# Second-block attention in head pairs: row halves for scores, scaled probabilities, values as the stationary operand on column halves

## The reference

```python
def global_gqa(q, k, v, k_ctx, v_ctx):            # layer 0, kind "G"
    ...
        sc = jnp.einsum('bqkgd,bnkd->bkgqn', q_blk, k_all).astype(jnp.float32) * scale
        p = jax.nn.softmax(sc, axis=-1).astype(v_all.dtype)
        return jnp.einsum('bkgqn,bnkd->bqkgd', p, v_all)

def windowed_gqa(q, k, v, k_ctx, v_ctx, sink_logit):   # layer 1, kind "W"
    ...
        p = jax.nn.softmax(jnp.concatenate([s_loc, s_ctx, s_sink], axis=-1), axis=-1)
    ...
# neighbourhood_attention, layer 1, kind "N": the same with a position bias and no sink
y = jnp.concatenate([y_a * jax.nn.silu(ag), y_b * jax.nn.silu(hg)], axis=-1)
x = x + gate[:, None] * jnp.matmul(y, w_out[layer])
```

## Time and profile before

| | us |
|---|---|
| median of 3 runs (1758.97 to 1762.38) | 1761.64 |
| span of the profiled execution | 1749.0 |
| TensorE (PE) busy | 1610.5 (92%) |
| VectorE (DVE) busy | 970.5 (55%) |
| ScalarE (ACT) busy | 785.3 (45%) |
| share of the chain that ended last: PE, DVE, ACT | 74%, 14%, 6% |
| mean granted TensorE clock | 0.956 |

### The profile page before, as it was taken

One profiled execution on the slowest core, in us unless ns is written; L12 is line 12 of the kernel. 1 busy time (PEld: TensorE's weight loads), 2 busy tenths in 40 slices (PEclk: granted clock), 3 DMA queues, 4 the chain that ended last, 5 costly groups with the idle time before them and its releaser, 6 DMA issues.

```text
span 1749.0 us, 20908 instructions
## 1 busy us (share of the span) xinstructions
PE 1610.5 (92%) x8012; PEld 1243.0 (71%) x8012; DVE 970.5 (55%) x1725; ACT 785.3 (45%) x1329; POOL 46.8 (3%) x105
## 2 busy tenths in 40 slices
PE   3899998799989999987999989999968999889997
PEld 3787777699878877776998717677733572676666
DVE  2554457566455544566664426744777731784664
ACT  2444785455344447854553314344420011533552
POOL 4000000000000000000000000000000000310000
PEclk8899999899999999988999999999979999898999
DMA  8653333476545532326665473311210025742000
GB/s 193 241 184 105 108 110 120 121 193 199 191 165 181 178 121 97 121 97 168 169 193 193 169 264 97 98 49 49 73 48 1 0 73 194 221 121 72 25 25 25
DMA packets 188838, 220.94 MB, mean 126 GB/s; under 512 B 20505, under 2 KB 117445, under 8 KB 188672
## 3 DMA queue, kind: packets, MB, share of 16 engines
q1 hardware_dynamic: 186532, 211.98, 38.2%
q0 software_dynamic: 2208, 7.63, 1.8%
HBM read 216.57 MB, written 3.01 MB: 126 GB/s over the span
## 4 chain that ended last, share of the span: by engine, by line
PE 74%; DVE 14%; ACT 6%; issue 3%; SPq 2%; DMA 0%; ACTq 0%; DVEq 0%
PE bank L570 19%; PE bank L572 18%; PE bank L571 18%; PE bank L835 5%; PE bank L896 2%; DVE w_low L1487 2%; SPq L2142 2%; ACT w_high L1125 2%; PE bank L922 2%; PE bank L907 2%; PE bank L730 1%; PE bank L676 1%; DVE arena L1800 1%; PE bank L707 1%; PE bank L1001 1%
## 5 line engine op out<-in xcount | busy, mean ns | idle before, releaser
L1487 DVE TENSOR_TENSOR w_low<-raw,w_high 128x1024 fp32r<-128x1024 f32 x352 | 424.9, 1217 | 422.0 <-ACT w_high L1125 421.0
L1125 ACT ACTIVATE w_high<-raw 128x1024 fp32r<-128x1024 f32 x352 | 366.6, 1046 | 338.0 <-PE bank L572 338.0
L570 PE MATMUL bank<-w_high,acts_r 128*128 128x512 f32 (+1 forms) x896 | 361.6, 404 | 45.6 <-DVE w_low L1487 22.6
L572 PE MATMUL bank<-w_high,acts_r 128*128 128x512 f32 (+1 forms) x896 | 351.4, 392 | 0.0
L571 PE MATMUL bank<-w_low,acts_r 128*128 128x512 f32 (+1 forms) x896 | 350.6, 391 | 0.0
L570 PEld LDWEIGHTS bank<-w_high,acts_r 128*128 128x128 f32 x896 | 173.4, 194 | 85.6 <-DVE w_low L1487 26.9
L570 PE MATMUL bank<-acts_r,w_high 128*128 128x256 f32 (+1 forms) x736 | 230.0, 313 | 0.0
L571 PE MATMUL bank<-acts_r,w_high 128*128 128x256 f32 (+1 forms) x736 | 223.6, 304 | 0.0
L572 PE MATMUL bank<-acts_r,w_low 128*128 128x256 f32 (+1 forms) x736 | 223.6, 304 | 0.0
L572 PEld LDWEIGHTS bank<-w_high,acts_r 128*128 128x128 f32 x896 | 172.6, 193 | 37.4
L571 PEld LDWEIGHTS bank<-w_low,acts_r 128*128 128x128 f32 x896 | 173.1, 193 | 32.6
(11 more groups left out here) (261 smaller groups left out, 1806.0 us busy)
## 6 DMA issues: line engine op xcount, KB each, us to landing
raw<-in_w_in SPq DMA_DIRECT2D x70, 1024.0 KB, 5.1
raw<-in_w_up SPq DMA_DIRECT2D x64, 512.0 KB, 5.5
raw<-in_w_down SPq DMA_DIRECT2D x32, 1024.0 KB, 4.8
raw<-in_w_ada SPq DMA_DIRECT2D x24, 1024.0 KB, 5.2
raw<-in_w_in SPq DMA_DIRECT2D x32, 512.0 KB, 4.9
raw<-in_w_o SPq DMA_DIRECT2D x8, 1024.0 KB, 5.0
raw<-in_w_out SPq DMA_DIRECT2D x8, 1024.0 KB, 4.9
raw<-in_w_out_c SPq DMA_DIRECT2D x4, 768.0 KB, 5.1
```

The lines of the kernel that those rows point to most:

```text
L570: mm(o, lh, rh, start=start, stop=False)
L572: return mm(o, ll, rh, start=False, stop=stop)
L1125: run(A_(high, src, ACT.Copy), (high_ready, n + 1))
L1487: run(V.tensor_tensor(low, src, high.bitcast(F32), ALU.subtract), (split_ready, n + 1))
```

## The change

Units come in pairs: two heads, one even and one odd, on the same tile. The step of the loop on each engine is now a pair. TensorE does both scores one behind the other (even head on rows 0 to 63 of its array, odd head on 64 to 127), then both turnings, then twice the features, then the values of pair p-2. There the values are stationary (128 x 64) and the turned probabilities move, 128 columns; the even head's output goes to partitions 0 to 63 and the odd head's to 64 to 127 of one bank, block by block in turn. The output has features on its partitions. VectorE multiplies the probabilities by the inverse of the sum in place (`scale_probs`) before they are turned, and TensorE waits for that (`probs_scaled`). ScalarE copies one output per pair. `turn_outputs` is gone, and VectorE multiplies by the gate from SBUF. `S` and `PT` have two buffers as before. Lines of the changed program have other numbers: L897 is the scores, L908 the turning, L927 the values, L1123 ScalarE's copy, L1350 the exponential of layer 0, L1116 the rounding, L1821 and L1823 the scaling.

```diff
@@ -150,8 +150,8 @@
 def units_of_block2(layer):
 
     if layer == 0:
-        return [("G", h, t) for h in range(QH) for t in range(T4)]
-    return [(k, h, t) for k in ("W", "N") for h in range(QH) for t in range(TILES)]
+        return [("G", 2 * hp + e, t) for hp in range(QH // 2) for t in range(T4) for e in range(2)]
+    return [(k, 2 * hp + e, t) for k in ("W", "N") for hp in range(QH // 2) for t in range(TILES) for e in range(2)]
 
 
 def half_list():
@@ -426,7 +426,8 @@
-        sum_inverted = Signal(sem("sum_inverted"), softs)
+        sum_inverted = Signal(sem("sum_inverted"), [k for k in b1u if kinds[k] != "C"])
+        probs_scaled = Signal(sem("probs_scaled"), b2u)
...
@@ -901,52 +902,44 @@
                     return range(2, 4) if kind == "G" and t >= TILES else range(4)
 
                 def second(u):
-                    pe.wait_ge(*probs_at(2 + l, u))
+                    pe.wait_ge(*probs_scaled.at(2 + l, u))
                     o = open_bank("p", 2 + l, u, 0, among=ATTENTION_BANKS)
                     for n, _ in enumerate(blocks_of(u)):
                         ins = tr(o[:, n * P:(n + 1) * P], S[:, u % 2, n * P:(n + 1) * P], ident[:, :])
                     close_bank(ins, "p", 2 + l, u, 0)
 
-                def values(u):
-                    kind, h, t = U[u]
-                    pe.wait_ge(*emptied("p", 2 + l, u, 0))
-                    o = open_bank("o", 2 + l, u, among=ATTENTION_BANKS)
-                    blocks = blocks_of(u)
+                def values(p):
+
+                    for u in (2 * p, 2 * p + 1):
+                        pe.wait_ge(*emptied("p", 2 + l, u, 0))
+                    o = open_bank("o", 2 + l, p, among=ATTENTION_BANKS)
+                    blocks = blocks_of(2 * p)
                     for n, b in enumerate(blocks):
-                        if kind == "G":
-                            v = kv2[:, b, (KVH + h // 4) * DH:(KVH + h // 4 + 1) * DH]
-                        elif kind == "W":
...
+                        for u in (2 * p, 2 * p + 1):
+                            kind, h, t = U[u]
+                            if kind == "G":
+                                v = kv2[:, b, (KVH + h // 4) * DH:(KVH + h // 4 + 1) * DH]
+                            elif kind == "W":
+                                v = kv3[:, b, (KVH + h // 4) * DH:(KVH + h // 4 + 1) * DH]
+                            else:
+                                v = nv[:, b, h * DH:(h + 1) * DH]
+                            half = DH * (h % 2)
+                            ins = mm(o[half:half + DH, 0:P], v, PT[:, u % 2, n * P:(n + 1) * P], start=n == 0, stop=n == len(blocks) - 1)
+                    close_bank(ins, "o", 2 + l, p)
+
+                pairs = len(U) // 2
+                for p in range(pairs + 2):
                     ended_in[(2 + l, "at")] = []
...
+                    if p < pairs:
+                        scores(2 * p)
+                        scores(2 * p + 1)
+                    if 1 <= p <= pairs:
+                        second(2 * p - 2)
+                        second(2 * p - 1)
+                    advance(filler, 2 * per_unit if p < pairs else 1000)
+                    if p >= 2:
+                        values(p - 2)
+                    ended_in[(2 + l, p)] = ended_in[(2 + l, "at")]
 
             def out2(l, tiles, first, second, ready=None):
                 acts = lambda k, t: tiles_of(first)(k, t) if k < 4 else tiles_of(second)(k - 4, t)
...
@@ -1338,36 +1329,34 @@
 
             def attention2(l):
                 U = units_of_block2(l)
...
+                pairs = len(U) // 2
+                for p in range(pairs + 2):
+                    if 1 <= p <= pairs:
+                        if p >= 2:
+                            act.wait_ge(*filled("o", 2 + l, p - 2))
+                        for u in (2 * p - 2, 2 * p - 1):
+                            n = (2 if U[u][0] == "G" and U[u][2] >= TILES else 4) * P
+                            copy_out(PT[:, u % 2, 0:n], bank("p", 2 + l, u, 0)[:, 0:n], "p", 2 + l, u, 0)
+                    if p < pairs:
+                        for u in (2 * p, 2 * p + 1):
+                            splits.due("s", 2 + l, u)
+                            kind, h, t = U[u]
+                            n = SEQ if kind == "G" and t >= TILES else N4
+                            if kind == "G":
+
+                                act.wait_ge(*bias_ready.at(2, u))
+                                if u >= 2:
+                                    act.wait_ge(*filled("p", 2 + l, u - 2, 0))
+                                run(A_(S[:, u % 2, 0:n], bank("s", 2, u)[:, 0:n], ACT.Exp, bias=stat[:, u % 4, 1, 0:1],
+                                       scale=SCALE, accum_out=stat[:, u % 4, 2, 0:1]), emptied("s", 2, u))
+                            else:
+                                softmax_exp(2 + l, u, n, S[:, u % 2, 0:n], kind, SCALE)
+                    for key in ended_in[(2 + l, p)]:
                         take_features(l, key)
...
+                    if p >= 2:
+                        kind, h, t = U[2 * p - 4]
+                        dst = {"G": o2_plain, "W": o3_plain, "N": y3_plain}[kind]
+                        copy_out(dst[:, h // 2, t * P:(t + 1) * P], bank("o", 2 + l, p - 2)[:, 0:P], "o", 2 + l, p - 2)
 
             act.wait_ge(*x_added.at(4))
             act.wait_ge(context_loaded, 16)
@@ -1821,17 +1810,21 @@
             def attention2(l):
                 U = units_of_block2(l)
 
-                def invert_sum(u):
+                def scale_probs(u):
                     st = stat[:, u % 4, :, :]
+                    kind, h, t = U[u]
+                    n = SEQ if kind == "G" and t >= TILES else N4
                     dve.wait_ge(*probs_at(2 + l, u))
-                    if U[u][0] == "W":
+                    if kind == "W":
                         run(V.tensor_tensor(st[:, 2, 0:1], st[:, 2, 0:1], st[:, 3, 1:2], ALU.add))
                         run.settle()
-                    run(V.reciprocal(st[:, 2, 1:2], st[:, 2, 0:1]), sum_inverted.by(2 + l, u))
-
-                for u in range(len(U) + 1):
-                    splits.due("s", 2 + l, min(u, len(U) - 1))
-                    if u < len(U):
+                    run(V.reciprocal(st[:, 2, 1:2], st[:, 2, 0:1]))
+                    run.settle()
+                    run(V.tensor_scalar(S[:, u % 2, 0:n], S[:, u % 2, 0:n], st[:, 2, 1:2], None, ALU.mult), probs_scaled.by(2 + l, u))
+
+                pairs = len(U) // 2
+                for p in range(pairs):
+                    for u in (2 * p, 2 * p + 1):
                         kind, h, t = U[u]
                         st = stat[:, u % 4, :, :]
                         n = SEQ if kind == "G" and t >= TILES else N4
@@ -1857,12 +1850,18 @@
                                                            op0=ALU.mult, op1=ALU.min), bias_ready.by(2 + l, u))
                             else:
                                 run(V.tensor_scalar(st[:, 1, 0:1], st[:, 0, 0:1], -SCALE, None, ALU.mult), bias_ready.by(2 + l, u))
-                    if u >= 1:
-                        invert_sum(u - 1)
-                        for key in ended_in[(2 + l, u - 1)]:
+                    splits.due("s", 2 + l, 2 * p + 1)
+                    if p:
+                        for key in ended_in[(2 + l, p - 1)]:
                             take_features(l, key)
-                for key in ended_in[(2 + l, len(U))]:
-                    take_features(l, key)
+                    for u in (2 * p, 2 * p + 1):
+                        scale_probs(u)
+                for p in range(pairs - 1, pairs + 2):
+                    for key in ended_in[(2 + l, p)]:
+                        take_features(l, key)
+                run.settle()
+                for p in range(pairs - len(ATTENTION_BANKS), pairs):
+                    dve.wait_ge(*emptied("o", 2 + l, p))
 
             def add_gated(l, n, tiles, gate_b):
                 for c in range(2):
@@ -2034,11 +2032,8 @@
             run(V.memset(no_mask, 0.0))
             run.settle()
             attention2(1)
-            for n, (key, x, gate) in enumerate((("o3", oT3, wgT), ("y3", yT3, ngT))):
-                for b in range(2):
-                    dve.wait_ge(*filled("oT", 3, 2 * n + b))
-                    run(V.tensor_tensor(x[:, 2 * b:2 * b + 2, :], bank("oT", 3, 2 * n + b)[:, :].rearrange("p (a n) -> p a n", a=2),
-                                        gate[:, 2 * b:2 * b + 2, :], ALU.mult), emptied("oT", 3, 2 * n + b))
+            for key, x, plain, gate in (("o3", oT3, o3_plain, wgT), ("y3", yT3, y3_plain, ngT)):
+                run(V.tensor_tensor(x, plain, gate, ALU.mult))
```

More of the change, by code:

```diff
@@ L314, in two_blocks @@
         fourier_fwd = carve(at, 2, 2, SEQ)
-        o2_tok = carve([q_at], T4, GW)
+        o2_plain = carve([q_at], QH // 2, N4)
         oT2 = carve([base], QH // 2, N4)
@@ L375, in two_blocks @@
         no_mask = carve(at, SEQ)
-        o3_tok = carve([wq_at], TILES, GW)
```

(13 more changed lines are left out.)

58 lines of the change are left out of this document (removed).

## The result

| | before | changed |
|---|---|---|
| median, same chip (4 runs each) | 1761.81 us | 1779.07 us |
| lowest to highest | 1758.97 to 1762.38 | 1775.53 to 1791.1 |
| span of the profiled execution | 1749.0 | 1773.7 |
| TensorE, VectorE, ScalarE busy | 1610.5, 970.5, 785.3 | 1574.0, 1000.3, 766.1 |
| mean granted TensorE clock | 0.956 | 0.949 |

The changed kernel takes 1.0137 times the time of before (95% interval 1.0088 to 1.0185); on a second chip it was 1.0120 (1.0075 to 1.0166), 1779.62 against 1758.58. The medians in the table alone give 1.0098, inside the interval. It is slower by 1.0 to 1.4%.

What follows compares the result with a forecast made beforehand. TensorE alone was taken to bound the first layer's attention and nearly so the second's. Terms +11.6 + 2 - 0.8 = +13, plus 4 for the clock, on 1761.6 gave 1779 us, range 1766 to 1801.

Steps and rivals of the forecast that it cites:

- Layer 0's ring, +11.6: First layer's attention: values, copies, exponentials, next scores, turning and features run serially, 41.5 against 37.9 us per four pairs: +11.6.
- 0.2 for a change of shape: First layer's serial sum: 0.2 us for a change of shape before the values, 0.8 over four pairs.
- the 0.21 of a score product: TensorE's score products: 0.21 us of each is the first load and the emptying, besides 0.84 per 512 columns.
- Nine slots for sixteen passes: Values' product: the halves overlap, 1.0 us with 512 keys, 0.54 with 256; bounds 0.84 (eight slots) and 1.7 (serial).
- named as a sign: Values' product: the prediction is right if the sixteen passes of a pair lie within 1.0 to 1.1 us.
- Layer 1, +2: Second layer's attention: turning waits for scaled probabilities, 6.7 and 7.2 us per pair against 6.66 and 6.92: +2.
- The clock, +4: First layer: a third of the seven longest lulls pull the clock down 3.4 us each, 1.7 lost a time: +4.
- The end, -0.8: Turning of outputs at the very end: VectorE's 1.50 us idle gives way to a 0.3 copy with wakes: -0.8.
- The 12.6 around the span: Whole kernel before: median 1761.64 us is 12.6 above the profiled execution's span of 1749.0, taken as unchanged.
- No overlap: Rival on the values' product: the array's halves do not overlap, +32 + 4, 1797 us; chance 0.2.
- Round trip covered: Rival on ScalarE's wait for the values: trip covered, TensorE sets the time, 1729 us; 0.1 including a no-change case.
- The clock falls with nearly every lull: Rival on TensorE's clock: +13 + 24, or more if the second layer joins, 1800 to 1815 us; chance 0.08.

Runs made afterwards that it cites:

- experiment 1: Changed kernel with ScalarE's two exponentials of a pair moved ahead of the copies, and the output copy ahead of the features: 1736.4 us, ratio 0.991 to before.
- experiments 1 and 4: The second of these: the kernel before with pair order alone, operands of the values as before, no scaling of probabilities: 1778.3 us, ratio 1.014 to before.
- experiment 2: Changed kernel with the passes of the values' product issued head by head, not block by block in turn: 1790.4 us, ratio 1.021 to before.
- experiment 6: Changed kernel with VectorE's two scalings of a pair moved ahead of the split and the features' work: 1779.6 us, ratio 1.013 to before.
- experiment 9: Changed kernel with the values' passes issued two blocks of one head, then two of the other, in turn: 1774.95 us, run once.
- experiment 8: Changed kernel with ScalarE's exponentials ahead of the copies and VectorE's scaling left out, outputs not divided by their sums: 1716.2 us, ratio 0.976 to before.
- experiment 10: Kernel before with pair order alone (operands as before, no scaling of probabilities) and ScalarE's exponentials ahead of the copies: 1724.7 us, ratio 0.982 to before.
- experiment 3: Changed kernel without VectorE's scaling, turning waits for the exponential alone, outputs not divided by their sums: 1754.3 us, ratio 1.000 to before.

## Why the prediction was right, and where it was not

The time, 1779, and the sign came out, and layer 0 by the mechanism forecast. But the clock's term was too small and stood in one layer only, and layer 1 had a ring I did not see. That the sum still met the median is luck.

- *Layer 0's ring, +11.6.* Steady rhythm 40.88 against 37.85: +3.03 per four pairs, 0.76 a pair (0.9 forecast). The layer grew by 14.9: two steps with half-clock stretches in them take 13.17 and 12.45, where the same shapes take 9.58 and 10.86 later on, 5.2 more, nearly all by the clock; about 10 is the ring. Shown by experiments 1 and 4. The sum's 0.2 for a change of shape is shown by no run, and none shows how the 0.21 of a score product divides. What the runs show in its place: from 1180 to 1250 the values' product starts 0.32 to 0.33 us behind the last feature product (seven times, loads of 128 x 64 behind 128 x 128), where before it started 0.23 to 0.24 behind it (fifteen times, 128 x 128 throughout): 0.09 more.
- *Nine slots for sixteen passes.* An estimate of mine, in the sum as 1.0 and 0.54, that no run shows. The runs show the two halves starting 7 ns apart and sixteen passes in eight slots, 16 loads in 0.85 us (8 in 0.42 with 256 keys). (The 1.09 of the product's row, which I had named as a sign, holds the last pass's own modelled length too, and can't tell eight slots from nine.) I had let the second head's first pass wait for the first head's second; in the changed kernel it did not, and in experiment 2 the second head's first pass started ahead of three of the first head's. The lower of the prediction's two bounds, eight slots in 0.84, was the better number. Nor did passes always start in the order of issue: in the 256-key product of experiment 2 the second head's first pass was issued fifth and started second, 13 ns behind the first.
- *Layer 1, +2.* At full clock right: 6.79 and about 7.0 against the forecast 6.7 and 7.2. But I had no second ring: the scaling's price was put at 0.6 per pair inside one chain, and taking it out gives 1.13. VectorE's features stand in that ring too, which would explain the difference; experiment 6 shows only that their place before or behind the scaling doesn't matter. The fourth step (10.46; 10.77 in experiment 9) lost more than the clock can: I had allowed 0.15 to 0.3 for what stands in front of the scalings, and there a split on VectorE had first to wait for ScalarE's rounding, and the turning waited 4.59 us:

```profile
1631.66 1.23 DVE L1476 TENSOR_TENSOR w_low<-raw,w_high 128x1024 fp32r<-128x1024 f32 x1 [2.09 <-ACT w_high L1116]
...
1636.18 1.97 PE L908 MATMUL bank<-ident,arena 128*128 128x128 f32 x8 [4.59 <-DVE arena L1823]
```

- *The clock, +4.* This term was mis-sized: "if a third of the seven longest" lulls of layer 0. Layer 0 lost 5.2, near enough. Layer 1, which I had left at nothing, went from 12.8 to 27.3 us at half clock, and the stretch behind it from 3.3 to 11.9. Two us at half clock hold the work of one (products 0.42 to 0.43 apart for 0.23), so this costs at most 7 and 4; the stretch behind grew by 2.2 in all. In layer 1 the four steps behind the fourth that hold one fall of 3.4 us each take 8.51, 8.16, 8.99 and 8.07, the one among them without a fall 6.92: 1.2 to 2.1 a time, against the term's 1.7; its 3.4 us a fall stands in no row of mine, but is the length of these falls. Between kernels a fall counts less: experiment 9 has 10.2 us less at half clock in layer 1 and is only 2.2 shorter; why is not shown. By these two rates (estimates) the clock took 3 to 6 of the 9.1 us that layer 1 grew by. The row that should have warned me was before's own clock in layer 1, 0.94: it fell there already. From 1640 to 1680 it is now 0.83.
- *The end, -0.8.* From the last load of the values to VectorE's multiplication: 1714.39 to 1716.00 before, 1736.88 to 1738.06 now, -0.4. The multiplication itself took 1.28 to 1.29 for two 512-wide rows from the banks, and takes 1.22 to 1.23 for one of 1024 from SBUF.
- *The 12.6 around the span.* Wrong. In every later result the run's time is 1.8 above its span, so the profiled execution of before took about 1750.8, 11 under the median: a fast one. The sum itself starts from the median and doesn't use the 12.6. But against that execution the changed kernel's is 24.7 longer (layer 0 14.9, layer 1 9.1, behind it 2.2, elsewhere -1.6), not 17. The medians differ by 17.3 on one chip and 21 on the other, and the ratio 1.0137 stands for 24 us (15 to 33 by its interval). So the terms were some 8 too low for the traces, mostly in layer 1 (9.1 against 2, by the clock and the fourth step), and the agreement to the microsecond with one chip's median is luck: single executions of one kernel differ by more than that, ahead of the attention.
- *Rivals.* "No overlap" is refuted by the passes (sixteen loads in 0.85 us; serially 1.7). "Round trip covered" is what experiment 1 builds: 1736 where I had put 1729, the missing part being layer 1's scaling (without it, 1716 in experiment 8). "The clock falls with nearly every lull" is refuted in layer 0, where it stays at 1.00 from 1180 to 1250 through seven waits of up to 1.9 us; layer 1 did join.

What stays open: why the granted clock falls in layer 1 at times and not at others (27.3 us twice in the changed kernel, 17.1 in experiment 9, whose steps are otherwise the same), and whether putting the scaling elsewhere than on VectorE would keep the halves' gain in layer 1; that wasn't tried, and by kernels 8 and 10 it has 1.7 us to win in this order.

## What to carry to other kernels

When two units become one step and the number of buffers stays, list for each engine what its first instruction of a step waits for: a wait that used to look a whole step back looks at the last instruction of the step before, and everything behind it on that engine (here the exponentials, 6.66 us idle) is serial from then on. Often the order on one engine mends it, without a buffer. And moving work to a half-idle engine is only free where that engine is not inside the ring: the same scaling cost nothing in layer 0 and 1.1 us a pair in layer 1.

## What the runs showed of the hardware

- Passes on two halves of the array ran together in the changed kernel: sixteen loads of 128 x 64 in 0.85 us, and 1.88 for the sixteen of 128 x 128 that do the same work in experiment 10.
- In experiment 2 a pass for the free half started ahead of three passes that waited for the other half, and not while four did: 0.013 us behind the first of four passes issued before it, 0.49 behind the first of eight.
- In layer 1 a step of the changed kernel with one 3.4 us fall of the granted clock to half in it took 1.2 to 2.1 us longer than the 6.92 of the one without. With the scaling gone from the same order (experiment 3) the time at half clock in layer 1 was 9.5 us instead of 27.3.
